# Two transfers of 256 columns for one of 512: the first rows of x at the start of a two-block kernel, with seven filler products for eight

## The reference

```
def rmsnorm(x, g):
    xf = x.astype(jnp.float32)
    y = xf * lax.rsqrt(jnp.mean(xf * xf, axis=-1, keepdims=True) + NORM_EPS)
    return (y * g.astype(jnp.float32)).astype(x.dtype)
...
for i in range(DEPTH):
    hn = rmsnorm(h, norm_g[i])
    ...
        q, k, v, z = split_proj(hn, w_in_a[j], N_KV_A)     # proj = h @ w_in
```

## Time and profile before

| what | value |
|---|---|
| median of three runs | 861.2 us |
| the profiled execution, its own time | 861.23 us |
| its span, first to last instruction | 859.3 us |
| around the span | 1.9 us |
| TensorE busy | 851.4 us, 99% of the span |
| VectorE, ScalarE, GpSimd busy | 66%, 59%, 14% |
| TensorE's share of the chain that ended last | 98% |

### The profile page before, as it was taken

How to read it: one execution, slowest core, us unless ns; L and a number is a source line. 1 busy time by engine, 2 the same in 40 slices (tenths; PEclk the granted TensorE clock), 3 DMA queues, 4 the chain that set the end, 5 groups by cost and what they waited for, 6 DMA issues and landing times.

```text
span 859.3 us, 12071 instructions
## 1 busy us (share of the span) xinstructions
PE 851.4 (99%) x4401; PEld 698.7 (81%) x4401; DVE 564.1 (66%) x1025; ACT 509.0 (59%) x929; POOL 122.3 (14%) x96
## 2 busy tenths in 40 slices
PE   9999999999999999999999999999999999999997
PEld 6877888778887888888888888877888888888885
DVE  6867866678776798655555446576797755555444
ACT  8667466766887864644444334787874644444332
POOL 0212053110152420000000000152330000000001
PEclk9999999999999999999999999999999999999999
DMA  9823563445534446665555555444347655665531
GB/s 328 281 58 136 177 203 119 148 147 177 167 126 147 127 134 205 220 195 181 175 186 194 195 196 173 151 145 145 104 145 220 215 178 175 191 196 186 188 115 50
DMA packets 94942, 146.15 MB, mean 170 GB/s; under 512 B 6564, under 2 KB 55204, under 8 KB 94884
## 3 DMA queue, kind: packets, MB, share of 16 engines
q1 hardware_dynamic: 92852, 139.58, 50.1%
q0 software_dynamic: 1296, 4.72, 1.6%
q10 hardware_dynamic: 736, 1.07, 0.3%
HBM read 144.32 MB, written 1.05 MB: 169 GB/s over the span
## 4 chain that ended last, share of the span: by engine, by line
PE 98%; DMA 0%; issue 0%; POOL 0%; DVE 0%; ACT 0%; SPq 0%; POOLq 0%; DVEq 0%
PE bank L1241 83%; PE bank L1151 7%; PE bank L1392 2%; PE bank L1320 1%; PE bank L1296 1%; PE bank L1293 1%; PE bank L1323 1%; DMA h<-in_x 0%; PE bank L1172 0%; PE bank L1167 0%; PE bank L1382 0%; PE bank L1399 0%; PE bank L1170 0%; PE bank L1360 0%; POOL scaled L1701 0%
## 5 line engine op out<-in xcount | busy, mean ns | idle before, releaser
L1060 DVE TENSOR_TENSOR lo<-raw,hi 128x1024 fp32r<-128x1024 f32 x242 | 296.2, 1254 | 96.2 <-ACT hi L1411 93.5
L1411 ACT ACTIVATE hi<-raw 128x1024 fp32r<-128x1024 f32 (+1 forms) x258 | 264.8, 1059 | 105.8 <-PE bank L1241 101.9
L1241 PE MATMUL bank<-hi,xT_hi 128*128 128x512 f32 (+2 forms) x720 | 282.6, 393 | 0.0
L1241 PE MATMUL bank<-hi,xT_lo 128*128 128x512 f32 (+2 forms) x720 | 276.3, 384 | 0.0
L1241 PE MATMUL bank<-lo,xT_hi 128*128 128x512 f32 (+2 forms) x720 | 275.5, 383 | 0.0
L1241 PEld LDWEIGHTS bank<-hi,xT_hi 128*128 128x128 f32 x720 | 135.3, 188 | 28.4 <-issue 4.3
L1241 PEld LDWEIGHTS bank<-hi,xT_lo 128*128 128x128 f32 x720 | 135.2, 188 | 27.3
L1241 PEld LDWEIGHTS bank<-lo,xT_hi 128*128 128x128 f32 x720 | 135.5, 188 | 24.2
L1241 PE MATMUL bank<-hi,hT 128*128 128x512 f32 x348 | 108.3, 390 | 0.0
L1241 PEld LDWEIGHTS bank<-hi,hT 128*128 128x128 f32 x348 | 65.3, 188 | 13.6
L1241 PE MATMUL bank<-lo,hT 128*128 128x512 f32 x174 | 67.7, 389 | 0.0
(11 more groups left out here) (269 smaller groups left out, 963.4 us busy)
## 6 DMA issues: line engine op xcount, KB each, us to landing
raw<-in_w_in SPq DMA_DIRECT2D x26, 1024.0 KB, 5.1
raw<-in_w_gate SPq DMA_DIRECT2D x44, 512.0 KB, 4.0
raw<-in_w_up SPq DMA_DIRECT2D x44, 512.0 KB, 5.0
raw<-in_w_down SPq DMA_DIRECT2D x22, 1024.0 KB, 4.9
raw<-in_w_out SPq DMA_DIRECT2D x20, 1024.0 KB, 5.1
raw<-in_w_in_b SPq DMA_DIRECT2D x10, 1024.0 KB, 5.1
raw<-in_w_in_a SPq DMA_DIRECT2D x7, 1024.0 KB, 8.0
raw<-in_w_in_a SPq DMA_DIRECT2D x8, 256.0 KB, 5.6
```

Of the source, the lines that this page charges most:

```text
L1060: return engine.tensor_tensor(lo[r][:, cols], raw[c.i % RAW][:, cols], hi[r][:, cols].bitcast(F32), ALU.subtract)
L1241: last = nc.tensor.matmul(bank[:, 0:wd], still[a], mv[r][:, off:off + wd], start=c.first and i == 0 and j == 0, stop=(c.last or c.closes a ...
L1411: nc.scalar.activation(hi[c.i % SPLIT][:, cols], raw[c.i % RAW][:, cols], ACT.Copy)\
```

## The change

The first transfer of SyncE's queue carries the columns 0 to 255 of x's first 128 rows, no longer 0 to 511. The columns 256 to 511 go out as the third transfer of ScalarE's queue, behind the identity and the gain rows, with a semaphore of their own, `x_second`. TensorE waits for it before b, and ScalarE before the squares of these rows. TensorE runs seven fillers at the start.

```
-            sp.dma_start(h[:, 0, 0:512], x[:, 0, 0:512]).then_inc(x_first[0], 16)
+            sp.dma_start(h[:, 0, 0:256], x[:, 0, 0:256]).then_inc(x_first[0], 16)
...
-        warmed(8)
+        warmed(7)
...
-                pe.wait_ge(x_in if s.n else x_first[s.m], 16)
+                pe.wait_ge(x_in if s.n else x_second if s.q and not s.m else x_first[s.m], 16)
...
         act.dma_start(gain_rows8[:, :], t["norm_g"][0].rearrange("(k p) -> k p", p=P)).then_inc(columns_in, 16)
+        act.dma_start(h[:, 0, 256:512], t["x"][0, 0:P, 256:512]).then_inc(x_second, 16)
...
                     act.wait_ge(x_in if s.n else x_first[s.m], 16)
+                    if s.n == 0 and s.m == 0:
+                        act.wait_ge(x_second, 16)
```

More of the change, by code:

```diff
@@ L1013, in build @@
     x_first = [nc.alloc_semaphore(f"x_first{m}") for m in range(M)]
+    x_second = nc.alloc_semaphore("x_second")
     piece_in = [nc.alloc_semaphore(f"piece_in{k}") for k in range(8)]
```

## The result

The changed kernel takes 862.43 us, the median of 15 runs, against 861.5 us for the kernel before beside it: a ratio of 1.0016, with a 95% interval of 1.0009 to 1.0023. The change makes the kernel 0.9 us slower in the median. The forecast of no change at 861.2 us was wrong, and its range, up to 861.7 us, did not hold the time. The runs of the changed kernel also lie far apart, 861.7 to 864.91 us; those of before lie between 861.16 and 862.07 us. The profiled execution of the changed kernel took 863.56 us.

A forecast was written before the change was run, and what follows sets the result against it. TensorE, at 98% of the chain, bounds the kernel, so only its stream's start counts. Piece 0's path adds 0 and the second rows' +0.08 us is hidden: 861.23 + 0 = 861.2 us, range 860.9 to 861.7.

The forecast's parts named there:

- a's load: TensorE's start: with one filler less, a's weight load comes near 3.9 us instead of 4.24 us.
- the table load: ScalarE's start: the added transfer issue moves the table load from 1.80 to about 2.2 us, at cost 0.
- the identity 0.4 us sooner (0.3 expected): First transfers: 1 KB packets let x and the identity through 0.3 us sooner, about 3.1 us behind issue.
- sooner a brings nothing by itself: TensorE's start: a at most 0.35 us sooner gains 0, since its reader ScalarE stands at piece 0 until 5.28 us.
- A: Rival at ScalarE's high part (4.74 us): piece 0 lands up to 0.29 us sooner; 861.1, at most 860.95; chance 0.18.
- B: Rival ahead of c: second half lands late, near 5.75 us, and b holds TensorE; 861.6 us; chance 0.22.
- C: Rival at the fillers: the removed one is where the clock rose; later rise slows first products; 862.6 us; chance 0.05.
- as late as 5.2 us: TensorE ahead of c: b may begin by 5.2 us at no cost, needing under 0.5 us before 5.65 us.
- it lands at 5.2 us, and costs nothing: Argument against late landing: judged by the identity's 3.4 us, the second half lands at 5.2 us, costing nothing.
- a follows at once: Argument against the clock rival: only about the last 0.1 us before the rise belonged to the removed filler.
- the sum had +-0: Path from piece 0 to the third head product: 0.09 us from packets running alone cancels 0.08 us of delay.
- The term of +0.08 us on the second rows: DMA engines: 16 packets of 47 ns replace 8 of 84 ns, landing the second rows 0.08 us later, hidden.

The follow-up runs named there:

- the lowest runs without the split: Kernel before (one 512-column transfer, eight fillers) with b also waiting for the second rows: lowest 861.72 us against 861.24, median 861.96, ratio 1.0006.

## Why the prediction was wrong

Right: a's load at 3.8 us and its transposes at 3.89 us; the table load at 2.18 us, hidden; the identity 0.4 us sooner (0.3 expected); and that sooner a brings nothing by itself. The signs that it named for being wrong appeared all three: hi of piece 0 at 4.34 us (A), b at 5.89 us with c right behind (B), and products 0.43 us apart behind 6 us (C). B's wait is what happened, and so is C's lower clock, but not by the missing filler alone, the cause that C gave.

The step that failed is the landing of the second half. I let b begin "as late as 5.2 us" at no cost, and took the identity's 3.4 us for the new transfer: "it lands at 5.2 us, and costs nothing". It took 4.05 us and landed at 5.84 us. The figure for B, the second rows' 3.95 us from 1.8 us, was there and nearly exact; I gave it 0.22. The identity was the wrong neighbour: it was the first of its queue. The second half, behind two others and beside piece 0 and the second rows, took about as long as the second rows did before; as second of its queue it still took 3.9 us.

The price of B was too small, and it was so because B and C stood as two cases with chances of their own. I priced B's wait at 0.3 to 0.45 us. The lowest runs of the changed kernel, 861.70 against 861.16 us, put the wait at 0.5 us, if the clock cost nothing in them (none of them was profiled), and the lowest runs without the split say the same. But the wait is idle time of TensorE ahead of the products, and by the profiles that is where C's lower clock came from. I looked for C's gap at the missing filler ("a follows at once", which it did) and not at b, where 1.16 us of idle time came. The median of 0.9 us holds both, and the highest run lies over 3 us above the kernel before. C's size was nearer: removing all fillers costs 1.0 us in the median, where I had 1.4 us.

A's mechanism occurred too: piece 0 was there 0.4 us sooner, where the sum had +-0. None of that could be used behind b. The term of +0.08 us on the second rows can't be read in these traces, since their landing varies by far more (3.7 to 5.6 us from issue with the same transfers).

The Trainium skill's page "TensorE: Matmul & The Clock Gate" (Part 1) says that the point at which the clock rises varies from run to run, by about half a microsecond. The two profiles without a gap, near 4 us in the kernel before and near 6 us with ten fillers, differ by more. What sets it in a given run stays open, and so does the split of the changed kernel's 0.9 us into wait, clock and a possible share of the split itself beyond the 0.5 us of its lowest run.

## What to carry to other kernels

A transfer split in two is worth what its last part allows: ask which in-order engine will stand at the second half, what is queued behind it, and take its landing from a transfer that was issued as late and shared the DMA engines with as many others. A wait that lies ahead of the first long stream of products can cost twice, once for itself and once for the clock where it hasn't risen yet, so the two aren't rivals with chances of their own but one case with a sum. Where runs differ by more than the effect, compare the lowest runs and the medians apart: the one points to the fixed wait, the other to what varies.

## What was not expected of the hardware

The landing of one transfer varies between runs of kernels that issue the same transfers in the same order: the second rows, issued at 1.65 us, landed at 5.3 us in the changed kernel's profile, at 5.55 us in that with b behind d, and at 7.25 us in that with b behind the head. In the last of these the clock fell some time after 2.11 us of idle time, when products were already running again at 2.4 GHz; the granted clock reads 0.54 in the mean from 8.9 to 12 us. And continuous work from 0.9 us on didn't fix the point at which the clock rose: 4 us in one profile, 6 us in another.
